# A two-layer hybrid decoder step: causal mask on VectorE, paired weight loads, stacked sample tokens, outputs one unit later

## The reference, cut to what matters

```python
ba, ca, xa, za, q, kc, vc, ks, vs, kw, vw, gbr, zb, gmix = _project(x, pos, ln_g[i], w_in[i])
u = ca * xa
conv_y, tail = _short_conv(u, prefix, conv_w[i])          # three taps
yb = nsa(q, kc, vc, ks, vs, kw, vw, gbr)                  # compressed + selected + window attention
x = _merge(x, ba * conv_y, za, yb, zb, gmix, p[i], ...)   # w_out_a, w_out_b, w_o, w_ple, w_ple_gate

def _masked_probs(s, mask):
    s = jnp.where(mask, s.astype(jnp.float32), NEG_INF)
    m = jnp.max(s, axis=-1, keepdims=True)
    e = jnp.where(mask, jnp.exp(s - m), 0.0)
    return e / jnp.maximum(jnp.sum(e, axis=-1, keepdims=True), 1e-30)
```

## Time and profile before

| what | us |
|---|---|
| median of three runs | 2334.16 |
| the profiled execution | 2328.78 |
| its span, first to last instruction | 2327.0 |
| PE busy | 2218.1 |
| DVE busy | 1448.6 |
| ACT busy | 998.3 |
| POOL busy | 220.0 |

### The profile page before, as it was taken

The page is one execution under the profiler, slowest core; times in us unless marked ns, Lnnn a source line. Parts: engine busy times, 40 slices in busy tenths (PEclk is TensorE's granted clock), DMA queues, the critical chain, the costliest instruction groups (busy, mean ns, idle before and its releaser), DMA issues.

```text
span 2327.0 us, 46865 instructions
## 1 busy us (share of the span) xinstructions
PE 2218.1 (95%) x18243; PEld 1992.8 (86%) x18243; DVE 1448.6 (62%) x2566; ACT 998.3 (43%) x1933; POOL 220.0 (9%) x357
## 2 busy tenths in 40 slices
PE   8999899999999899999989989999999999998997
PEld 8999899999989455589989989999998985554997
DVE  5888455446786666554478866554567756666544
ACT  4333233525554555532343323334446446555232
POOL 0000001000000333310000000000000003334000
PEclk9999999999999999999999999999999999999999
DMA  7554466844211876753345644777052237669431
GB/s 244 165 156 138 130 183 165 199 125 149 98 67 37 139 126 115 152 170 101 111 149 154 186 118 119 218 186 212 25 185 91 74 37 127 110 112 222 144 96 39
DMA packets 405540, 312.73 MB, mean 134 GB/s; under 512 B 224281, under 2 KB 376281, under 8 KB 404040
## 3 DMA queue, kind: packets, MB, share of 16 engines
q1 hardware_dynamic: 399752, 268.70, 46.4%
q0 software_dynamic: 5568, 41.05, 4.8%
HBM read 282.80 MB, written 77.09 MB: 155 GB/s over the span
## 4 chain that ended last, share of the span: by engine, by line
PE 71%; DVE 11%; ACT 4%; DMA 4%; SPq 3%; issue 3%; DVEq 2%; POOL 1%; ACTq 0%; POOLq 0%
PE ps L1004 28%; PE ps L992 9%; PE ps L1177 8%; PE ps L1256 5%; PE ps L1420 3%; PE ps L1277 3%; PE ps L1444 2%; PE ps L1403 2%; DMA w_raw<-in_w_in 2%; PE ps L1202 2%; PE ps L1542 2%; SPq L688 2%; POOL pr L934 1%; ACT pr L2157 1%; PE ps L1691 1%
## 5 line engine op out<-in xcount | busy, mean ns | idle before, releaser
L456 DVE TENSOR_TENSOR wL<-w_raw,wH 128x2048 fp32r<-128x2048 f32 (+1 forms) x77 | 177.0, 2298 | 123.1 <-ACT wH L450 122.9
L1004 PE MATMUL ps<-hH,wH 128*128 128x272 f32 x1088 | 225.6, 289 | 1.3 <-DVE wL L456 1.2
L1004 PE MATMUL ps<-hH,wL 128*128 128x272 f32 x1088 | 226.2, 289 | 0.0
L1004 PE MATMUL ps<-hL,wH 128*128 128x272 f32 x1088 | 224.8, 288 | 0.0
L934 POOL TENSOR_SCALAR pr<-pr,inv,zg 128x512 f32<-128x512 f32 (+3 forms) x256 | 156.4, 621 | 552.6 <-DVE inv L2975 552.3
L1004 PEld LDWEIGHTS ps<-hH,wH 128*128 128x128 f32 x1088 | 171.4, 189 | 2.5 <-DVE wL L456 2.4
L1004 PEld LDWEIGHTS ps<-hH,wL 128*128 128x128 f32 x1088 | 170.9, 189 | 0.0
L1004 PEld LDWEIGHTS ps<-hL,wH 128*128 128x128 f32 x1088 | 170.6, 188 | 0.0
L475 ACT ACTIVATE wpH<-w_raw 128x512 fp32r<-128x512 f32 x168 | 102.0, 623 | 158.7 <-DMA w_raw<-in_w_in 84.8
L450 ACT ACTIVATE wH<-w_raw 128x2048 fp32r<-128x2048 f32 (+1 forms) x77 | 147.7, 1918 | 44.9 <-DMA w_raw<-in_w_in 23.2
L1256 PE MATMUL ps<-chH,w1H 128*128 128x256 f32 x512 | 148.0, 289 | 0.0
(11 more groups left out here) (415 smaller groups left out, 5868.3 us busy)
## 6 DMA issues: line engine op xcount, KB each, us to landing
w_raw<-in_w_in SPq DMA_DIRECT2D x59, 1024.0 KB
rows_keep<-in_cache_kv SPq DMA_DIRECT2D x256, 128.0 KB, 4.0
craw<-rows_keep SPq DMA_DIRECT2D x32, 1024.0 KB, 7.3
w_raw<-in_w_in SPq DMA_DIRECT2D x64, 256.0 KB
k_sel<-in_cache_kv SPq DMA_DIRECT2D x128, 128.0 KB, 5.1
v_sel<-in_cache_kv SPq DMA_DIRECT2D x128, 128.0 KB, 8.8
out_new_win_sample<-in_state_win POOLq DMA_DIRECT2D x16, 1016.0 KB, 5.3
w_raw<-in_w_out_a SPq DMA_DIRECT2D x8, 1024.0 KB
```

What stands on the lines that cost most here:

```text
L456: dve.tensor_tensor(block_part(wL, b), block_part(w_raw, b), block_part(wH, b).bitcast(F32), ALU.subtract).then_inc(w_lo, 1)
L1004: last = nc.tensor.matmul(ps[:, bank + hf, 0:HALF], st, x[:, k, hf * HALF:(hf + 1) * HALF], start=k == 0 and w is wH and x is xH, stop=k = ...
```

## The change

1. **Causal mask.** `mk` becomes a float32 table of 128 x 512 that is loaded directly. The four mask matmuls of a unit and ACT's cast of the mask go. `maxima` becomes two DVE instructions (one for each group), each of which adds the mask to the scores, negates the sum, writes the result to `pr` and gives the minimum of it, that is, the negated maximum. `exps` then works in place in `pr` with scale -1. `scores(i+2)` and `key_tp` wait for `pa_nm` instead of `pa_exp`, and the wait for `pa_t` moves from `exps` to `maxima`.
2. **Outputs.** `output(i-1)` of iteration i becomes `output(i-2)`; at the first unit of a block of eight both are issued, at the second none; the last two follow the loop.
3. **Loads.** In the first 32 blocks the two loads of a pair of blocks follow each other, and then four pages of keys and two of values are copied.
4. **Token sums.** `token_sums` moves to the end of block 1 on DVE, and `tokens_high` to the end of block 1 on ACT; `token_lows` moves to block 2, and `both_taps(0)` to block 3, among the pieces of block 4.
5. **Sample parts.** DVE copies the high and the low part of the 32 sample tokens side by side (`hS`, 64 columns). The sample tile of a TM block takes 16 matmuls (high and low weights) instead of 24; the low half of the result is copied by ACT (`z_low`) and added by DVE (`sample_rows`); ACT's sigmoid of the sample gates follows that (`sample_gates_in`), one block later.
6. `w_sum` moves to another place in SBUF, and the load of the final gain signals another semaphore.

```diff
@@ load order @@
-                            regroup_some(l, 2, 1)
+                            if n % 2:
+                                regroup_some(l, 4, 2)
...
                     load_w(l, B_MA + 2 * i, w_cols("w_in", l, C_MIX + BW * i))
-                    regroup_some(l, 2, 1)
                     load_w(l, B_MA + 2 * i + 1, w_cols("w_out_a", l, BW * i))
-                    regroup_some(l, 2, 1)
+                    regroup_some(l, 4, 2)
@@ TM blocks on PE @@
+                        if tt == NT:
+                            pe.wait_ge(tm_sample, (TM_BLOCKS + 1) * l + i + 1)
+                            for k in range(KT):
+                                for w in (wH, wL):
+                                    last = nc.tensor.matmul(ps[0:2 * NSAM, NT, 0:width], hS[:, k, :], w[:, n, k, 0:width],
+                                                            start=k == 0 and w is wH, stop=k == KT - 1 and w is wL)
+                            last.then_inc(tile, 1)
+                            continue
@@ scores @@
-                        pe.wait_ge(pa_exp, UNITS * l + i - 1)
+                        pe.wait_ge(pa_nm, UNITS * l + i - 1)
                     for rows, bank in sides:
-                        nc.tensor.matmul(ps[:, bank, 0:n], qT[rows, REP * gp + r, u * P:n], kT[rows, br, gp, 0:n], start=True, stop=False)
-                    for half in range(2):
-                        for rows, bank in sides:
-                            last = nc.tensor.matmul(ps[:, bank, u * P:n], mk[rows, half, 0, :], mk[rows, half, 1, :], start=False, stop=half == 1)
+                        last = nc.tensor.matmul(ps[:, bank, 0:n], qT[rows, REP * gp + r, u * P:n], kT[rows, br, gp, 0:n], start=True, stop=True)
@@ unit loop on PE @@
-                    if i:
+                    if i and k == 0:
+                        output(i - 2)
                         output(i - 1)
+                    elif k > 1:
+                        output(i - 2)
@@ ACT, block 1 @@
-                            if i == 0 and kind == 2 and jj == 0:
+                        if i == 0 and kind == 1:
                                 tokens_high(...)   # four times
@@ sample gates on ACT; in the tile loop @@
+                def sample_gates_in(i):
+                    act.wait_ge(tm_sample, (TM_BLOCKS + 1) * l + i + 2)
+                    act.activation(zg[0:NSAM, NT, 8 * i:8 * i + 8], z_low[:, KV:WW], ACT.Sigmoid)
+                    act.drain()
...
+                        if tt == NT:
+                            act.activation(z_low[:], ps[NSAM:2 * NSAM, NT, 0:WW], ACT.Copy).then_inc(tm_ev, 1)
+                            continue
@@ exps @@
-                    if i >= 3:
-                        act.wait_ge(pa_t, UNITS * l + i - 2)
-                        last = act.activation(pr[i % 3][:, g, 0:n], ps[:, 2 * (i % 2) + g, 0:n], ACT.Exp, bias=nmx[:, i % 3, g:g + 1],
+                        last = act.activation(pr[i % 3][:, g, 0:n], pr[i % 3][:, g, 0:n], ACT.Exp, bias=nmx[:, i % 3, g:g + 1], scale=-1.0,
@@ DVE, conv @@
-                        if i and kind == 3:
+                        if kind == 3:
                             dve.drain()
                             ahead(b + 1, lambda: both_taps(i))
-                        elif b == 3:
-                            ahead(b + 1, token_lows)
...
                             shifted(0, 1)
+                            token_sums()
                         elif kind == 2:
-                            token_sums()
-                            both_taps(0)
+                            token_lows()
@@ sample_rows and maxima on DVE @@
+                def sample_rows(i):
+                    dve.wait_ge(tm_ev, nth(tm_ev, l * (5 * TM_BLOCKS) + 5 * i + 5))
+                    z, c0 = ((zc, 0), (zc, KV), (zkk, 0), (zkk, KV), (zv, 0), (zv, KV))[i]
+                    dve.tensor_tensor(z[0:NSAM, NT, c0:c0 + KV], ps[0:NSAM, NT, 0:KV], z_low[:, 0:KV], ALU.add)
+                    dve.tensor_tensor(z_low[:, KV:WW], ps[0:NSAM, NT, KV:WW], z_low[:, KV:WW], ALU.add).then_inc(tm_sample, 1)
...
-                    dve.tensor_reduce(out=nmx[:, i % 3, :], in_=ps[:, b:b + 2, 0:P * (unit(i)[2] + 1)], op=ALU.max, axis=AX.X, negate=True
-                                      ).then_inc(pa_nm, 1)
+                    if i >= 3:
+                        dve.wait_ge(pa_t, UNITS * l + i - 2)
+                    for g in range(2):
+                        last = dve.tensor_tensor_reduce(out=pr[i % 3][:, g, 0:n], in0=ps[:, 2 * (i % 2) + g, 0:n], in1=mk[:, SEQ - n:SEQ], scale=-1.0,
+                                                        scalar=-NEG, op0=ALU.add, op1=ALU.min, accum_out=nmx[:, i % 3, g:g + 1])
+                    last.then_inc(pa_nm, 1)
```

More of the change, by code:

```diff
@@ L147, in turn_tables, with causal_mask @@
     return np.ascontiguousarray(both.astype(np.float32).reshape(P, 2 * TOK))
-def mask_halves():
+def causal_mask():
     q = np.arange(P)
-    eye, causal = np.eye(P, dtype=np.float32), np.where(q[:, None] >= q[None, :], 0.0, NEG).astype(np.float32)
-    half = [np.stack([eye[64 * h:64 * h + 64], causal[64 * h:64 * h + 64]], 1) for h in range(2)]
-    both = np.stack(half, 1).reshape(64, 4 * P)
-    return np.ascontiguousarray(np.concatenate([both, both], 0))
+    return np.where(q[:, None] + SEQ - P >= np.arange(SEQ)[None, :], 0.0, NEG).astype(np.float32)
 def build(nc, a):
@@ L198, in build @@
         grow = fixed("grow", [P, 4, 3])
-        mk = fixed("mk", [P, 2, 2, P], BF16)
+        mk = fixed("mk", [P, SEQ])
         pages = fixed("pages", [1, NSEQ * NPAGE], I32)
@@ L618, in build @@
         FROM_PE = ["rows 4", "gain", "rows 0", "rows 1", "scaled sample"] + ["chunk %d" % c for c in range(KT)] + ["rows 2", "rows 3", "columns"]
-        FROM_ACT = ["root 4", "root 0", "root 1", "root 2", "root 3", "high sample", "high weights", "rows 1", "rows 2", "rows 3", "masks"]
+        FROM_ACT = ["root 4", "root 0", "root 1", "root 2", "root 3", "high sample", "high weights", "rows 1", "rows 2", "rows 3"]
         FROM_DVE = ["scaled 4", "rows 4", "gain", "scaled 0", "scaled 1", "sample", "scaled 2", "rows 0", "scaled 3",
@@ L1638, in _ @@
                         turn_back(mm)
+                output(UNITS - 2)
                 output(UNITS - 1)
@@ L1878, in _ @@
                                 act.activation(halves(cv_in[:, 3, jj, :]), bank, ACT.Sigmoid).then_inc(cv_sg, 1)
-                            if i == 0 and kind == 2 and jj == 0:
-                                tokens_high(quarter(tX, 0, 0), quarter(tXr, 0, 1), 0)
-                                tokens_high(quarter(tM, 0, 1), quarter(tMr, 1, 1), 1)
-                                tokens_high(quarter(tX, 1, 0), quarter(tXr, 1, 1), 2)
-                                tokens_high(quarter(tM, 0, 0), quarter(tMr, 1, 0), 3)
-                        if l + i == 0 and kind == 1:
-                            act.activation(mk[:].rearrange("p h k q -> p (h k q)"), mk_raw[:], ACT.Copy).then_inc(start_act, 1)
+                        if i == 0 and kind == 1:
+                            tokens_high(quarter(tX, 0, 0), quarter(tXr, 0, 1), 0)
+                            tokens_high(quarter(tM, 0, 1), quarter(tMr, 1, 1), 1)
+                            tokens_high(quarter(tX, 1, 0), quarter(tXr, 1, 1), 2)
+                            tokens_high(quarter(tM, 0, 0), quarter(tMr, 1, 0), 3)
                 for i in range(4):
@@ L2744, in _ @@
                         make_low(dve, l, b + 1)
+                    if i:
+                        sample_rows(i - 1)
+                        dve.drain()
                     if i == 1:
```

37 lines of the change are left out of this document (20 added, 17 removed).

## The result

| | before | after | ratio, 95% interval |
|---|---|---|---|
| median of the runs, us | 2333.39 | 2297.31 | 0.9845 [0.9828, 0.9862] |
| profiled execution, its span | 2328.78, 2327.0 | 2295.55, 2293.8 | |

The change makes the kernel 36.1 us faster (32 to 40 by the interval); 2299 was forecast. The sum came out, but two of its terms did not, and one of the prices inside them did not either.

What follows compares the result with a forecast made beforehand. PE, busy for 95% of the span, was taken as the bound, with a chain across engines in the attention. Terms -11.6 - 13.3 + 0.9 - 10.8 = -34.8 us gave 2299 us on the median, range 2289 to 2309.

Steps and rivals of the forecast that it cites:

- Sample parts: TM blocks: 16 instead of 24 matmuls in each sample tile, all on PE's path, -11.6 us over both layers.
- the junction: From TM blocks to compression: ACT's last sigmoid some 0.9 us later, hidden by 64 prompt matmuls, taken as 0.
- Loads: Second load of a pair issued ahead of the page numbers: PE's waits of 6.9 and 6.4 us go, -13.3 us.
- Rival (c): Page loads: the late load only moves, as 22.5 us of SP delay the next pair; 2313 us, chance 0.07.
- Token sums: Moved token sums: -1.8 us in layer 0, +2.7 in layer 1, together +0.9, between -5 and +5.
- the wait at the fifth product: Block 4, both layers: sign that PE would wait about 3.5 us there, in layer 0 replacing the token-sum wait.
- Mask and outputs: Attention: mask matmuls and output waits go only in part, -5.4 us a layer, -10.8 in all, bounds -35 and +20.
- The quiet block: Attention block of eight units without sample work: 18.8 us instead of 19.8, a gain of about 1.0.
- step blocks: Five attention blocks a layer with a sample step: -0.4 us each, and 0.2 gained in the step itself.
- Three quiet blocks at -1.0: Attention: the blocks without a sample step, about 1.0 us gained in each, -3.0 a layer.
- DVE's price: Attention: two accumulating DVE instructions for one maximum, 0.35 us dearer in a unit, between +0.155 and +0.565.
- Rival (a): Attention: DVE becomes the bound, so it gains 0 or loses up to 10 us; 2315 us, chance 0.17.

Runs made afterwards that it cites:

- filler: Kernel after the change plus useless repeated score matmuls in the first attention block of each layer: 2292.16 us, ratio 0.9817 to the kernel before.
- best: Kernel after the change plus useless matmuls in first and last attention blocks, layer 1's token sums in their old place: 2282.83 us, ratio 0.9786 to the kernel before.

## Why the prediction was right

**Right in sum.** -34.8 forecast, -33.2 on the spans.

- *Sample parts*: -11.6 forecast, -11.6 measured (83.77 for 89.56 us, twice), no stall, the junction hidden.
- *Loads*: mechanism right, the term mis-sized: -13.3 forecast, -19.3 in the pair of traces and 18.3 when undone. The two waits were priced without the half clock behind them (1.7 and 2.3 us, 4.0 together), and a third place (waits of 1.17 and 0.40 us at full clock, 2.0 in all) was not looked for. Rival (c), the late load only moves, is excluded.
- *Token sums*: +0.9 forecast, +0.3 measured (-2.1, +2.4); the wait at the fifth product is there in both layers, 2.57 us where "about 3.5" was written. Where the clock falls behind it, as it did 15 times of 20, the move costs 1.1 to 1.3 us more in a layer, and then it is a loss over both.
- *Mask and outputs*: this step failed: -10.8 forecast, -3.5 measured. The quiet block (-0.9 for -1.0) and most step blocks (about -0.8 for -0.6) held. "Three quiet blocks at -1.0" took the first block as one of them; it lost 3.5 and 1.4 us, because the clock was lower in it. That the clock makes it long is shown by filler, best and the windows. That the missing mask matmuls let the clock fall is argued from PE's longer waits, not shown: the clock falls in some traces with the mask on PE too. The last block gave -0.5 and +1.0. The end, from the last turn to the gates, cost +1.2 and +0.6 where +0.5 was forecast (the prediction's own sum takes 0.6): two outputs at half clock.
- *DVE's price*, inside that term: 0.35 us in a unit taken, 0.08 measured, as the read and the next instruction overlap. Even the lower bound, +0.155, was too high. ACT's exponential had no term: from SBUF its row is 711 ns for 512 elements, from PSUM it was 685. With the right price the forecast for the attention would have been larger, and further off.
- Rival (a), DVE the bound, is excluded: DVE's busy time grew by 5.5 us in a layer's attention, not by 36. But the distance is small: one more maximum in a unit costs 29 us.

Most of the attention's shortfall of 7.3 us (4.5 and 2.4 in the first blocks) and 4.0 of the loads' surplus of 6.0 have the same cause with opposite signs, the clock. The short stalls (+1.7) and the compression (+2.2) were forecast as nothing, and small differences elsewhere (-3.0) offset part of them. That the forecast came within 2 us is thus partly luck.

## What to carry to other kernels

Price a wait of TensorE with what follows it: read the granted clock in windows of 1 us behind the longest waits, and add the slow stretch where there is one (here 1.7 and 2.3 us behind waits of 6.9 and 6.4, 1.1 to 1.3 behind 15 of 20 waits of 2.57, nothing behind one of 1.17). Read what an instruction costs an engine from one start to the next, and not from the sum of rows: two pairs of rows that add up to 1.54 us took 1.31. Before matmuls are taken away from a stage in which TensorE already waits for a chain, ask whether its clock will hold; where it doesn't, useless matmuls in front of the longest waits can pay (3.4 us for 28 matmuls). And when two edits uncover each other's wait, try them together: 0.29 and 0.19 us apart, 0.90 together.

## What the runs showed of the hardware

- The same wait of 2.57 us left the clock at 1.00 five times and at 0.50 for about 3 us fifteen times: one profile is no proof that a wait of this length is free. "TensorE: Matmul & The Clock Gate" of the Trainium skill (Part 1: The HAM clock gate) describes two levels, the lower as the default and the higher as released by activity. The trace agrees as far as it goes: behind the wait of 6.9 us the clock is 0.50, and it returns to 1.00 while PE works without a gap.
- DVE's accumulating instruction with a PSUM and an SBUF source runs at 687 ns for 512 elements, as without accumulator (688). Its read has a row of 83 ns (ACT's has 205), but the next instruction starts at the same time as the read (854.31 above), 0.62 us behind the start of the first.
- PE shows as fully busy at half clock (1.00 us of 1.00 with 6 matmuls instead of 10): the busy share hides this loss.
